# The identity of a blocked inverse added on VectorE, its copies on ScalarE, and one order of steps per engine

## The reference

```python
def step(state, inp):
    r_t, w_t, k_t, v_t, kk_t, a_t = inp
    sa = jnp.einsum('bhvk,bhk->bhv', state, -kk_t)
    state = (state * w_t[:, :, None, :]
             + sa[..., None] * (kk_t * a_t)[:, :, None, :]
             + v_t[..., None] * k_t[:, :, None, :])
    y_t = jnp.einsum('bhvk,bhk->bhv', state, r_t)
    return state, y_t

_, y = lax.scan(step, state0, (tm(r), tm(decay), tm(k), tm(v), tm(kk), tm(a)))
```

## Time and profile before

| | us |
|---|---|
| median of 3 runs | 3169.24 |
| lowest and highest | 3167.71 and 3170.28 |
| the profiled execution | 3181.79 |
| its span, first to last instruction | 3180.6 |
| the recurrence's products in it (L2295) | 1939.6 to 2318.4 |

### The profile page before, as it was taken

The page is one execution under the profiler, slowest core; times in us unless marked ns, Lnnn a source line. Parts: engine busy times, 40 slices in busy tenths (PEclk is TensorE's granted clock), DMA queues, the critical chain, the costliest instruction groups (busy, mean ns, idle before and its releaser), DMA issues.

```text
span 3180.6 us, 52988 instructions
## 1 busy us (share of the span) xinstructions
PE 2852.8 (90%) x22282; PEld 2293.8 (72%) x22282; DVE 1611.3 (51%) x2854; ACT 1053.1 (33%) x2008; POOL 635.5 (20%) x483
## 2 busy tenths in 40 slices
PE   7999889699999999969999987988878899999877
PEld 6776667578888888747778855878756678766655
DVE  3425565634444444467555415666545433377744
ACT  3214444411111111263322122444454222255552
POOL 2103233410011100035211101212102201122113
PEclk9997999899999999989999996999989899999988
DMA  3111013111111111112211210000032201101042
GB/s 101 51 47 40 27 41 126 33 47 47 53 48 40 53 47 53 53 34 86 80 34 41 63 55 2 4 30 4 4 107 73 93 27 42 36 31 40 27 135 90
DMA packets 200333, 162.65 MB, mean 51 GB/s; under 512 B 5232, under 2 KB 173850, under 8 KB 199586
## 3 DMA queue, kind: packets, MB, share of 16 engines
q1 hardware_dynamic: 200098, 159.26, 16.4%
HBM read 137.19 MB, written 22.05 MB: 50 GB/s over the span
## 4 chain that ended last, share of the span: by engine, by line
PE 74%; DVE 11%; ACT 6%; issue 5%; DMA 2%; POOL 2%; SPq 0%; DVEq 0%; ACTq 0%; POOLq 0%
PE ps L725 15%; PE ps L727 14%; PE ps L726 14%; PE ps L2295 7%; PE ps L1843 3%; PE ps L1767 3%; PE ps L1834 2%; PE ps L1469 2%; PE ps L1471 1%; PE ps L1470 1%; ACT r L685 1%; PE ps L777 1%; DVE r L690 1%; PE ps L779 1%; PE ps L778 1%
## 5 line engine op out<-in xcount | busy, mean ns | idle before, releaser
L725 PE MATMUL ps<-r,r 128*128 128x512 f32 (+1 forms) x2304 | 936.9, 407 | 96.7 <-DVE r L690 56.3
L726 PE MATMUL ps<-r,r 128*128 128x512 f32 (+1 forms) x2304 | 907.3, 394 | 0.0
L727 PE MATMUL ps<-r,r 128*128 128x512 f32 (+1 forms) x2304 | 906.1, 393 | 0.0
L725 PEld LDWEIGHTS ps<-r,r 128*128 128x128 f32 x2304 | 441.4, 192 | 229.5 <-DVE r L690 65.2
L671 POOL TENSOR_TENSOR sb<-sb 128x1024 f32<-128x1024 f32 x138 | 276.2, 2007 | 1296.6 <-DMA sb<-in_w_ffn_up 483.2
L726 PEld LDWEIGHTS ps<-r,r 128*128 128x128 f32 x2304 | 442.2, 192 | 94.0 <-issue 7.8
L727 PEld LDWEIGHTS ps<-r,r 128*128 128x128 f32 x2304 | 440.8, 191 | 94.0
L690 DVE TENSOR_TENSOR r<-sb,r 128x1024 fp32r<-128x1024 f32 x198 | 272.2, 1382 | 233.8 <-ACT r L685 233.5
L2295 PE MATMUL ps<-sb 64*64 64x64 f16 (+2 forms) x10368 | 300.7, 214 | 45.2 <-issue 27.5
L2295 PEld LDWEIGHTS ps<-sb 64*64 64x64 f16 (+1 forms) x10368 | 285.5, 125 | 70.5 <-issue 49.6
L685 ACT CAST r<-sb 128x1024 fp32r<-128x1024 f32 x198 | 204.9, 1043 | 213.9 <-POOL sb L671 213.8
(11 more groups left out here) (267 smaller groups left out, 3511.1 us busy)
## 6 DMA issues: line engine op xcount, KB each, us to landing
sb<-in_w_out SPq DMA_DIRECT2D x36, 512.0 KB, 4.0
sb<-in_a_w_in SPq DMA_DIRECT2D x29, 512.0 KB, 4.0
sb<-in_w_ffn_gate SPq DMA_DIRECT2D x22, 512.0 KB, 3.9
sb<-in_w_ffn_up SPq DMA_DIRECT2D x22, 512.0 KB, 3.9
sb<-in_w_ffn_down SPq DMA_DIRECT2D x22, 512.0 KB, 3.6
sb<-in_w_in SPq DMA_DIRECT2D x17, 512.0 KB, 4.1
sb<-in_x SPq DMA_DIRECT2D x16, 512.0 KB, 5.3
xs<-sb SPq DMA_DIRECT2D x4, 2048.0 KB, 9.4
```

The lines of the kernel that those rows point to most:

```text
L725: pe.matmul(self.out, w.hi[:, q, self.cols], hi, start=(q == 0), stop=False)
L726: pe.matmul(self.out, w.hi[:, q, self.cols], lo, start=False, stop=False)
L727: ins = pe.matmul(self.out, w.lo[:, q, self.cols], hi, start=False, stop=(q == w.nk - 1))
```

## The change

The identity is no longer a product. VectorE adds it while it copies X0 and each W from PSUM to f16; Xt0 is made by VectorE from level 0 in SBUF, with no product at all. X and Xt of every level are copied by ScalarE. VectorE's masks of `lr` are cut the other way: first the strict half of both banks (part 0), then the half with the diagonal (part 1), and the f16 copy waits for part 0 alone. The `ak` masks and levels 1 to 5 become a step of their own. In place of one `PERIOD` there is one list per engine.

```diff
-    PERIOD = "S A S A L S A L S P P A B A P B P E B E A B B E A B E"
-
-    def order(self):
+    ORDER = {
+        "PE": "S E A S L A S L A S P B A P A P P B A B A B A E E B E",
+        "DVE": "S A L A L A S A S E S P P B P A B P B A E A B B E E A",
+        "ACT": "B S A S S L A L S A P E A A P P P E A B A B B B E A E",
+        "POOL": "P S B B L B B E E A B B L A B E P P S B A S S B P A E",
+    }
+
+    def order(self, engine):
...
-            for c in self.PERIOD.split():
+            for c in self.ORDER[engine].split():
...
     def products_pe(self, pe, m):
-        k.free[0] = k.free[1] = ("lr", m)
+        k.free[0] = k.free[1] = ("lr", (m, 1))
...
     def products_dve(self, dve, m):
-        dve.tensor_tensor(self.lr[i][:, 0:3, :], self.bank(0, 3, 2 * CH), self.m3, ALU.mult)
-        dve.tensor_tensor(self.lr[i][:, 3:6, :], self.bank(1, 3, 2 * CH), self.m3, ALU.mult).then_inc(*s.lr.up(m))
+        both = k.ps[:, 0:2, 0:6 * CH].rearrange("p c (a b) -> p c a b", a=3)
+        masked = self.lr[i].rearrange("p (c a) b -> p c a b", c=2)
+        for part, mask in ((0, k.up), (1, k.upi)):
+            cols = slice(part * CH, part * CH + CH)
+            over = mask.unsqueeze(1).unsqueeze(1).broadcast_to((P, 2, 3, CH))
+            dve.tensor_tensor(masked[:, :, :, cols], both[:, :, :, cols], over, ALU.mult).then_inc(*s.lr.up((m, part)))
         dve.wait_ge(*s.inv_l.at(m))
         self.split_levels(dve, m, 0, 1)
+        yield
         dve.wait_ge(*s.p_ak.at(m))
...
         self.split_levels(dve, m, 1, 6)
-        yield
...
     def products_act(self, act, m):
-        act.wait_ge(*s.lr.at(m))
+        act.wait_ge(*s.lr.at((m, 0)))
...
     def inverse_pe(self, pe, m):
-        self.heads(pe, b, BT, CH, [(level[0], eyes), (eyes, eyes)]).then_inc(*s.i_x.up((m, 0)))
-        pe.wait_ge(*self.freed(bt))
-        self.heads(pe, bt, BT, CH, [(eyes, level[0]), (eyes, eyes)]).then_inc(*s.i_xt.up((m, 0)))
-        k.free[b], k.free[bt] = ("inv_x", (m, 0)), ("inv_xt", (m, 0))
+        self.heads(pe, b, BT, CH, [(level[0], eyes)]).then_inc(*s.i_x.up((m, 0)))
+        k.free[b] = ("inv_x0", m)
...
-            pe.wait_ge(*s.inv_x.at((m, lev - 1)))
+            pe.wait_ge(*(s.inv_x.at((m, lev - 1)) if lev > 1 else s.inv_x0.at(m)))
             pe.wait_ge(*self.freed(b))
-            self.heads(pe, b, BT, CH, [(level[lev], x16), (eyes, eyes)]).then_inc(*s.i_w.up((m, lev)))
+            self.heads(pe, b, BT, CH, [(level[lev], x16)]).then_inc(*s.i_w.up((m, lev)))
...
-            pe.wait_ge(*s.inv_xt.at((m, lev - 1)))
+            pe.wait_ge(*(s.inv_xt.at((m, lev - 1)) if lev > 1 else s.inv_xt0.at(m)))
...
     def inverse_dve(self, dve, m):
-        dve.wait_ge(*s.i_x.at((m, 0)))
         if m > 1:
             dve.wait_ge(*s.i_fix.at(m - 2))
-        dve.tensor_copy(self.x16[i], self.bank(b)).then_inc(*s.inv_x.up((m, 0)))
+        dve.wait_ge(*s.levels.at((m, 0)))
+        dve.tensor_tensor(self.xt16[i], self.levels16[i][:, 0], eyes, ALU.add).then_inc(*s.inv_xt0.up(m))
+        dve.wait_ge(*s.i_x.at((m, 0)))
+        dve.tensor_tensor(self.x16[i], self.bank(b), eyes, ALU.add).then_inc(*s.inv_x0.up(m))
         yield
         for lev in range(1, 6):
+            dve.wait_ge(*s.i_w.at((m, lev)))
+            dve.tensor_tensor(self.w16[i], self.bank(b), eyes, ALU.add).then_inc(*s.inv_w.up((m, lev)))
             yield
-            dve.wait_ge(*s.i_x.at((m, lev)))
-            dve.tensor_copy(self.z[i] if lev == 5 else self.x16[i], self.bank(b)).then_inc(*s.inv_x.up((m, lev)))
             yield
...
     def inverse_act(self, act, m):
-        act.wait_ge(*s.i_xt.at((m, 0)))
-        act.copy(self.xt16[i], self.bank(bt)).then_inc(*s.inv_xt.up((m, 0)))
         yield
         for lev in range(1, 6):
-            act.wait_ge(*s.i_w.at((m, lev)))
-            act.copy(self.w16[i], self.bank(b)).then_inc(*s.inv_w.up((m, lev)))
             yield
+            act.wait_ge(*s.i_x.at((m, lev)))
+            act.copy(self.z[i] if lev == 5 else self.x16[i], self.bank(b)).then_inc(*s.inv_x.up((m, lev)))
             act.wait_ge(*s.i_xt.at((m, lev)))
             act.copy(self.xt16[i], self.bank(bt)).then_inc(*s.inv_xt.up((m, lev)))
```

More of the change, by code:

```diff
@@ L2234, in order, with run_parts @@
         return out
-    def run_parts(self, make):
+    def run_parts(self, engine, make):
         parts = {}
-        for part, m in self.order():
+        for part, m in self.order(engine):
             if (part, m) not in parts:
@@ L2259, in pe @@
             k.free[b] = ("kk_normed", BT - 1)
-        self.run_parts(dict(L=lambda m: self.low_rank_pe(pe, m), E=lambda m: self.elementwise_pe(pe, m), P=lambda m: self.products_pe(pe, m),
+        self.run_parts("PE", dict(L=lambda m: self.low_rank_pe(pe, m), E=lambda m: self.elementwise_pe(pe, m), P=lambda m: self.products_pe(pe, m),
                             I=lambda m: self.inverse_pe(pe, m), S=lambda m: self.state_pe(pe, m)))
     def act(self, act):
-        self.run_parts(dict(L=lambda m: self.low_rank_act(act, m), E=lambda m: self.elementwise_act(act, m), P=lambda m: self.products_act(act, m),
+        self.run_parts("ACT", dict(L=lambda m: self.low_rank_act(act, m), E=lambda m: self.elementwise_act(act, m), P=lambda m: self.products_act(act, m),
                             I=lambda m: self.inverse_act(act, m), S=lambda m: self.state_act(act, m)))
@@ L2277, in dve @@
         dve.memset(self.st, 0.0).then_inc(*s.state.up(-1))
-        self.run_parts(dict(L=lambda m: self.low_rank_dve(dve, m), E=lambda m: self.elementwise_dve(dve, m), P=lambda m: self.products_dve(dve, m),
+        self.run_parts("DVE", dict(L=lambda m: self.low_rank_dve(dve, m), E=lambda m: self.elementwise_dve(dve, m), P=lambda m: self.products_dve(dve, m),
                             I=lambda m: self.inverse_dve(dve, m), S=lambda m: self.state_dve(dve, m)))
     def pool(self, pool):
-        self.run_parts(dict(L=lambda m: self.nothing(2), E=lambda m: self.elementwise_pool(pool, m), P=lambda m: self.products_pool(pool, m),
+        self.run_parts("POOL", dict(L=lambda m: self.nothing(2), E=lambda m: self.elementwise_pool(pool, m), P=lambda m: self.products_pool(pool, m),
                             I=lambda m: self.nothing(13), S=lambda m: self.nothing(4)))
@@ L2537, in inverse_dve @@
     def inverse_dve(self, dve, m):
-        s, i = self.s, m % 2
-        b, bt = 4 + 2 * i, 5 + 2 * i
-        dve.wait_ge(*s.i_x.at((m, 0)))
+        k, s, i = self.k, self.s, m % 2
+        b, eyes = 4 + 2 * i, over_pairs(k.eye16)
         if m > 1:
             dve.wait_ge(*s.i_fix.at(m - 2))
-        dve.tensor_copy(self.x16[i], self.bank(b)).then_inc(*s.inv_x.up((m, 0)))
+        dve.wait_ge(*s.levels.at((m, 0)))
+        dve.tensor_tensor(self.xt16[i], self.levels16[i][:, 0], eyes, ALU.add).then_inc(*s.inv_xt0.up(m))
+        dve.wait_ge(*s.i_x.at((m, 0)))
+        dve.tensor_tensor(self.x16[i], self.bank(b), eyes, ALU.add).then_inc(*s.inv_x0.up(m))
         yield
         for lev in range(1, 6):
+            dve.wait_ge(*s.i_w.at((m, lev)))
+            dve.tensor_tensor(self.w16[i], self.bank(b), eyes, ALU.add).then_inc(*s.inv_w.up((m, lev)))
             yield
-            dve.wait_ge(*s.i_x.at((m, lev)))
-            dve.tensor_copy(self.z[i] if lev == 5 else self.x16[i], self.bank(b)).then_inc(*s.inv_x.up((m, lev)))
             yield
```

## The result

| | us |
|---|---|
| kernel before, median of 4 | 3169.76 |
| changed kernel, median of 4 | 3139.03 |
| ratio, 95% interval | 0.9902, 0.9886 to 0.9918 |
| the changed kernel's profiled span | 3130.9 |

The gain is 30.7 us; the forecast was 25. The two profiled spans lie 49.7 apart, more than the medians do, since 8.6 us of the difference lie ahead of the stage (first product at 1939.6 and 1931.0). With a second profiled execution of each kernel the stage by itself, first to last product, is 378.8 and 377.6 us before, 340.6 and 343.4 after: 34 to 38 us less in pairs, where the interval of the medians is 26 to 36. Behind the stage little moved (862 and 861, 859 and 861).

What follows compares the result with a forecast made beforehand. TensorE was taken as held up by waits for copies and late code; 0.5 from order and levels plus 0.87 from code per period, times 13, plus 7 for fill and drain, gave 25 us: 3144, range 3122 to 3164.

Steps and rivals of the forecast that it cites:

- fill and drain: Start and end of the stage: three more chunk times with levels alone on the path, 7 us gained.
- the sum: Whole stage: 0.5 + 0.87 = 1.37 us per period, 17.8 over 13, with fill and drain 25 us.
- The walk of the new order: Steady period with the new lists, step by step: 19.3 us without low-rank steps, 21.1 with them, mean 20.2.
- The walk of the old order: Steady period in the old list by the same steps: 20.0 us, 21.4 with low rank, mean 20.7.
- order and operations: Steady period: new order and lighter levels give 0.5 us per period.
- The code: TensorE's "issue" idle is instructions arriving late; of 1.67 us per period about 0.8 stay, 0.87 returned.
- The adds: VectorE's identity adds on x0 and the five W's: 0.55 us each; Xt0 0.36.
- adds are dear: Rival: VectorE's adds take 0.71 us each, 16 us lost in all, 3163 to 3169, no change; chance 0.08.
- The masks: Chain from `lr` to x0: l16 starts 0.47 us earlier, Xt0's 0.36 stands ahead of x0; net about -0.1.
- The clock rival: Thinner f16 part brings half clock on TensorE: one more 3.4 us stretch per period eats the gain, two give 3195; chance 0.08.
- It doesn't do what it says: Rival: removed TensorE matmuls had hidden behind weight loads, so nothing would go; no chance given.

Runs made afterwards that it cites:

- e3: Kernel before, with the identity as one f16 matmul of 384 columns per call instead of twelve of 64 by 64; 3161.9 us, ratio 0.9974.
- e5: Changed kernel with the identity product back for x0 and the five W's, one matmul of 384 columns per call, plain VectorE copies; 3144.1 us, ratio 0.992.
- one list: Changed kernel's operations with the old single list of steps on all four engines; 3190.9 us, ratio 1.0069 to the kernel before.
- the run with the later copy: Changed kernel, but ScalarE's f16 copy waits for both mask operations instead of the first; 3144.5 us, ratio 0.992 to the kernel before.
- two moves: Changed operations, old list, but x5 behind w1 on TensorE and its copies later, x1's copy before the exponentials on ScalarE; 3177.2 us, ratio 1.0028.
- three moves: As with two moves, plus VectorE's decay and scan ahead of the state update and ScalarE's exponentials right behind the f16 copy; 3149.5 us, ratio 0.9918.

## Why the prediction was right

*The sign and the size.* 30.7 us measured for 25 forecast, well inside the range. The steady period came to 20.6, though, not to 21.6: 13 of them gave 28 to 31 us where 17.8 were forecast, and fill and drain 5 to 8 for 7. So the sum was 10 us and more too low in the steady part, and the medians, 6 us above the forecast, show less of that than the traces. The runs give a path of three steps with a time at each: less code in the old order, with the wide products' extra work (e3), 8 us; then lists, ScalarE's copies, the masks and Xt0 from SBUF (e5), 18; then the wide products gone, 5, with overlapping intervals.

*The walk of the new order.* Held almost to the tenth: 19.3 forecast without low-rank steps, and 19.1 to 19.3 between `lr` starts in six of the seven such periods (20.3 in the seventh); 21.1 with them, measured 21.3 to 21.7, but for the one beside the 2 MB load of the gates (24.3). x0, `g`, `add`, `fix` and the head sum are waited for where the walk put it; `fix` by 0.74, with 0.73 forecast. One of its sums doesn't come out of its own terms: 3.08 and 1.0, 1.15, 0.36 and 0.55 are 6.14, not 5.85. The 5.85 is right all the same, since VectorE's operations overlap: in the changed kernel x0's add (from 2143.60, 0.55 us) ends 2.73 us behind the first level (from 2141.06, 0.36), which makes 5.81.

*The walk of the old order.* This term was mis-sized. It gave 20.7 on average; 23.0 less 1.45 of code stops leaves 21.5. The sum took the difference for the same on both sides, and so it dropped out. Part of it is the clock: 0.97 over 299 us is five stretches of 3.4 us at half clock (from 1998, 2042, 2100, 2117 and 2274 us), at most 8.5 us of work, 0.7 a period. The forecast held the clock for unchanged; it went to 1.00. Apart from code stops a period fell from 21.5 to 20.2, by 1.4, of which the clock can be 0.7; so order and operations brought at least 0.7, where 0.5 was forecast.

*The code.* Right as a mechanism: the stops end behind the landing of code, and e3 took them away and gained time with more work for TensorE. The steps to its size were off. The 2.5 us for the densest block are a misreading: the 1.24 us lie ahead of 2178.61, not inside the 3.78 behind it, and the block's work there is 3.31. No row shows the 2.5, so the step from 1.24 to 0.7, by which the sum scales all stops, has no ground. "Issue" was read as code throughout; it is also where a wait for a copy lands when the profile can't name it (1.60 ahead of x5 with one list). Counted within calls, code fell from 1.45 to 0.46 a period, by 0.99, where 1.67 to 0.8 were forecast, by 0.87; it came that near by luck. Whether a microsecond of code is a microsecond of time, as the sum has it, isn't shown: 17.6 us fewer stops went with 9 to 11 less in the old order, 12.2 fewer with 5.9 in the new, but both times work for TensorE came in and clock came back.

*The adds.* 553 and 551 ns for 550, Xt0 351 for 360. The rival "adds are dear" falls.

*The masks.* "Net about -0.1" was too little: the run with the later copy shows 0.46 a period, because the 0.36 of Xt0 beside it stands behind the level masks, where x0 on TensorE is already under way.

*The clock rival.* It didn't come true in the changed kernel and did with one list, at 3191 where the rival said 3195. But its trigger was wrong. Not the 96 matmuls that are gone: the runs with one list, with two moves and with three all lack them, at 0.90, 0.95 and 1.00. Half clock in most periods is seen only in the two in which the order makes TensorE stand still for 1.6 us and more at one point of the fast part (12 and 9 of the 13 periods); single stretches also come in the kernel before and in five other runs.

*"It doesn't do what it says"* falls: 8832 matmuls remain of 10368, as counted.

*What was not seen.* That the operations need the lists. The prediction costed the new walk with the lists as given and never asked what the moved copies would do in the old one, where they cost 21 us.

## What to carry to other kernels

When a copy moves from one engine to another, its place in that engine's order moves too: cost it behind what will stand ahead of it, or the operation that saves work makes the kernel slower. In a part made of many small instructions count the instructions as well as the work; one matmul of 384 columns in place of twelve of 64 gave 8 us, although it is more work for TensorE. And price what an experiment puts in from its own trace, not only what it takes out: the wide product was taken for the same work and cost 0.2 us a call more, so it can't tell how much of the code's time came back.

## What the runs showed of the hardware

Code for TensorE arrived too slowly for dense stretches of f16 products of 64x64: one block of 126 matmuls took 3.78 us where its work was 3.31, and stops inside calls stood 126 matmuls or a multiple of it apart in the kernel before, within two. 25 stops of 0.16 us and more became 3 when 77 matmuls of a chunk's 648 went.

The 2 MB load of the gates went with late code. In each of the 14 traces the longest pause between the starts of two code packets in the 13 periods overlaps that load, 7.1 to 9.2 us where the median before is 4.2; the longest code stop of the kernel before (4.06 us) and of the changed one (2.63) ends behind the packet that was late.

In the run with two moves a stop of 1.91 us between two calls at 2.4 GHz was followed by 3.4 us at 1.2 GHz, in which the 48 matmuls of `rhs` took 2.5 us for 1.4. Stops of 0.95 and 0.97 in one period of the run with three moves weren't.

15% of the steady part hung on the order of steps, and with it on the clock: the same instructions took 315 us with one list and 268 with four.
